# Mixer of a two-layer block: separate VectorE signals, and banded heads normalized by a product with a diagonal in eleven turns

## The chip, the cores and the metric

The kernel runs on one core of one Trainium2 chip. The metric is the device time of one execution in microseconds (us); the time of a version is the median of its timed runs. All data is fp32 (in the large matrix products as pairs of rounded halves).

## What is computed

The program is a chain of two blocks. The first block (a diagonal state space layer, a gating unit, a routed layer of experts) comes first and isn't touched. The second block has two layers; its first layer begins with a mixer of two parts that read the same projections:

```
# part A, delta heads: 4 heads of 128, two directions, 5 chunks of 106 or 104 tokens in this kernel
a_mat = where(strict, (k*beta) @ k.T * decay, 0)          # decay = exp(gc_i - gc_j)
sol   = triangular_solve(I + a_mat, [v*beta, k*beta*exp(gc)])   # u, w
v_new = u - w @ S
o     = (q*exp(gc)) @ S + (q @ k.T * decay) @ v_new
S     = S * exp(gc_last) + k_dec.T @ v_new

# part B, banded heads: 8 heads of 64, 5 query tiles (16 meta tokens, then 4 of 128)
s = q @ k_window.T - slope * dist ; s_meta = q @ k_meta.T ; s_sink
p = softmax([s, s_meta, s_sink])
o = p_window @ v_window + p_meta @ v_meta
```

An output projection, an MLP and a second attention layer with its MLP follow.

## The kernel before

All five engines run one program written out by hand; semaphores join them. The mixer is four generators on each engine: one for each direction `d` of the delta heads and one for each of two banded heads that go side by side (`NWIN` = 2). `mixer_order()` (L1608) gives the order in which every engine advances them, the same on all: 125 steps, each with one turn of direction 0 and one of direction 1, and spread between them 8 x 20 window turns, each for both banded heads. Each of the 5 chunks of a direction takes 25 steps (numbered 0 to 24 here), so that direction 0 goes from the first chunk to the last and direction 1 the other way. A `yield` ends a turn. An engine does its turns strictly in this order: what waits holds up all that is queued behind it on that engine.

One chunk of a direction, by step:
- 0: TensorE sums the log decays and spreads them (L1641 to L1644, banks A and B); VectorE copies them (L2375, L2376), ScalarE takes two Exp (L1999, L2000), VectorE multiplies (L2378).
- 1: TensorE transposes k and v (L1650), ScalarE copies them (L2003, L2004), GpSimd makes vb, kbe and kd (L2265 to L2267).
- 2: VectorE makes the decay exponents Dm and DT (L2385, L2386, eight instructions), ScalarE takes three Exp (L2008 to L2010).
- 3: TensorE multiplies k by k and k by q (L1656, L1658); VectorE multiplies Dm, DT, qd and copies gl (L2394 to L2397), one signal behind them all; TensorE transposes A (L1663); ScalarE copies it (L2013).
- 4: VectorE starts the inverse Xi and its transpose XT (L2401 to L2407), one signal behind both; GpSimd masks A (L2277).
- 5 to 21: six rounds of doubling, each in three steps. TensorE multiplies the masked A by Xi (L1672), ScalarE copies the product T1 (L2018), in the next step TensorE updates (L1678 for Xi, L1681 for XT) and VectorE subtracts (L2414, L2416), one signal behind both. The third step is free.
- 22: U and W (L1686, L1688), copied by ScalarE (L2022, L2023). 23: the state is applied (L1695, L2422). 24: output and new state (L1702 to L1707, L2430 to L2439).

One pair of banded heads, by its 8 turns: 0, scores on TensorE (L1724, or L1727 and L1728). 1, VectorE adds the distance term and takes the maximum (L2457 to L2461). 2, ScalarE Exp with the sum (L2040). 3, VectorE reciprocal (L2465), ScalarE multiplies the weights by it (L2043). 4, TensorE transposes the weights with the identity (L1733, and L1734 for the 16 meta keys). 5, ScalarE copies them (L2047, L2048). 6, value products on TensorE (L1740, L1741). 7, VectorE copies the result out (L2471); the next pair's scores use the same bank and wait for that.

In the rows `GW_value` is the working space of direction 0, `delta` that of direction 1, `held_uH_value` the banded heads' space, `PS` the PSUM banks, `held_C` constants, `BIG` the projections and results. A product of fp32 is recorded as two MATMULs, a transpose as one.

## Time and profile before

| | us |
|---|---|
| median of three timed runs | 3447.63 (3445.48 to 3459.86) |
| the profiled execution's own time | 3457.6 |
| its span, first to last instruction | 3455.8 |
| the mixer in it | 1915 to 2352, 437 |
| busy in the whole span: TensorE, VectorE, ScalarE, GpSimd | 2829.4, 1703.9, 1677.4, 1126.7 |
| mean granted TensorE clock, as a share of 2.4 GHz | 0.871 |

The profile is of one execution. Busy time counts instructions of an engine; "idle before, releaser" is the time an engine stood idle before an instruction and the instruction whose signal let it go. A row that merges several instructions shows their count; the time in it runs from the start of the first to the end of the last, and instructions overlap by some 0.1 us. `PE` is TensorE, `PEld` its weight loads, `DVE` VectorE, `ACT` ScalarE, `POOL` GpSimd.

### The profile page before, as it was taken

How to read it: one execution, taken by the hardware profiler on the slowest of the kernel's cores; microseconds unless marked ns; L12 is line 12 of the kernel's file. 1: busy time of each engine (PE TensorE's matmuls, PEld its weight loads, DVE VectorE, ACT ScalarE, POOL GpSimd, SP SyncE). 2: the span in 40 equal slices, each digit the busy share in tenths (PEclk: the TensorE clock that was granted, in tenths of full speed). 3: DMA queues.
4: the chain of work that ended last, by engine and by line, in shares of the span. 5: the costliest groups of instructions: out<-in, count | busy, mean ns of one | idle time of the engine just before them, and what ended most of it. 6: DMA issues, size and time to landing. Idle time of an engine off the chain costs nothing.

```text
span 3455.8 us, 44071 instructions
## 1 busy us (share of the span) xinstructions
PE 2829.4 (82%) x17284; PEld 2378.8 (69%) x17284; DVE 1703.9 (49%) x3905; ACT 1677.4 (49%) x3352; POOL 1126.7 (33%) x877
## 2 busy tenths in 40 slices
PE   6577777777778776587589888888999999989999
PEld 4465566555656565455387776777999987778887
DVE  7596868685868678355353444543200123621010
ACT  2176676767676867588533232333322322533231
POOL 0033333333333333233132222223555532046463
PEclk8798888788887887589799788978999999999999
DMA  5298999999998999999122000001233321023332
GB/s 183 98 418 333 351 413 407 346 386 405 402 374 353 401 419 408 414 405 388 52 68 68 1 1 1 1 1 50 74 92 92 92 74 56 1 67 95 95 97 74
DMA packets 287522, 695.73 MB, mean 201 GB/s; under 512 B 27664, under 2 KB 207299, under 8 KB 221651
## 3 DMA queue, kind: packets, MB, share of 16 engines
q0 software_dynamic: 73728, 536.90, 38.8%
q1 hardware_dynamic: 213587, 156.02, 14.2%
q8 instruction: 136, 2.23, 0.3%
q14 instruction: 71, 0.58, 0.0%
HBM read 689.72 MB, written 3.15 MB: 200 GB/s over the span
## 4 chain that ended last, share of the span: by engine, by line
PE 54%; DVE 23%; DMA 11%; ACT 10%; issue 3%; POOL 0%; SPq 0%; DVEq 0%; ACTq 0%; POOLq 0%
PE PS L1771 28%; DMA ring<-in_peer_uv,eidx 10%; DVE ring L1494 6%; PE PS L906 5%; ACT ring L1111 3%; PE PS L783 2%; PE PS L960 2%; PE PS L1672 2%; PE PS L1681 2%; PE PS L1678 1%; PE PS L1793 1%; DVE W L1305 1%; DVE acc L2583 1%; PE PS L1970 1%; PE PS L1740 1%
## 5 line engine op out<-in xcount | busy, mean ns | idle before, releaser
L906 PE MATMUL PS<-C,ring 128*128 128x128 f32 x4096 | 711.5, 326 | 358.0 <-ACT ring L1111 357.1
L906 PEld LDWEIGHTS PS<-C,ring 128*128 128x128 f32 x4096 | 564.9, 167 | 521.2 <-ACT ring L1111 477.3
L711 POOL DMA_INDIRECT ring<-in_peer_uv,eidx x512 | 485.9, 949 | 1162.5 <-PE PS L906 982.8
L1494 DVE CUSTOM_DVE_ANT_0 ring<-ring,PS 128x1024 f32<-128x1024 f32 x512 | 619.5, 1215 | 314.2 <-DMA ring<-in_peer_uv,eidx 305.8
L1111 ACT ACTIVATE ring<-ring,act_d 128x512 f32<-128x512 f32 x1024 | 683.5, 714 | 16.7
L1771 PE MATMUL PS<-held_uH,GW 128*128 128x264 f32 (+1 forms) x3008 | 663.2, 315 | 20.8 <-POOL BIG_value L2308 16.8
L2294 POOL TENSOR_TENSOR GW<-held_wr,GW 128x1024 fp32r<-128x1024 f32 x178 | 428.7, 2410 | 437.0 <-ACT GW L2063 437.0
L1771 PEld LDWEIGHTS PS<-held_uH,GW 128*128 128x128 f32 x3008 | 504.4, 194 | 62.6 <-issue 17.4
L1771 PE MATMUL PS<-BIG_value,GW 128*128 128x264 f32 (+1 forms) x1504 | 448.5, 314 | 0.0
L1771 PE MATMUL PS<-hid,GW 128*128 128x264 f32 (+1 forms) x2304 | 366.5, 321 | 0.0
L1771 PEld LDWEIGHTS PS<-hid,GW 128*128 128x128 f32 x2304 | 332.3, 188 | 33.7
L1771 PEld LDWEIGHTS PS<-BIG_value,GW 128*128 128x128 f32 x1504 | 291.9, 194 | 14.8
L2063 ACT CAST GW<-held_wr 128x1024 fp32r<-128x1024 f32 x178 | 185.3, 1043 | 232.0 <-DVE BIG L2534 116.3
L1104 ACT ACTIVATE act_d<-act_d 128x1 f32<-128x1 f32 x512 | 101.7, 199 | 362.1 <-DVE act_d L1494 360.5
L2534 DVE TENSOR_TENSOR BIG<-BIG,PS 128x528 f32<-128x528 f32 (+1 forms) x48 | 33.4, 696 | 394.8 <-PE PS L1771 394.8
L2545 DVE TENSOR_TENSOR value<-BIG,PS 128x528 f32<-128x528 f32 (+1 forms) x64 | 44.5, 696 | 316.9 <-ACT BIG L2118 316.9
L1108 ACT ACTIVATE act_d<-act_d,gate 128x1 f32<-128x1 f32 x512 | 150.8, 295 | 18.8 <-ACT act_d L1104 0.4
L2308 POOL TENSOR_TENSOR hid<-value,hid 128x528 fp32r<-128x528 f32 (+1 forms) x64 | 83.9, 1311 | 132.8 <-ACT hid L2094 132.8
L2118 ACT ACTIVATE BIG<-PS 128x528 f32<-128x528 f32 (+1 forms) x64 | 38.8, 606 | 177.8 <-PE PS L1771 177.8
L2308 POOL TENSOR_TENSOR BIG_value<-BIG,held_uH 128x528 fp32r<-128x528 f32 (+1 forms) x28 | 37.0, 1326 | 168.2 <-ACT held_uH L2094 168.2
L2018 ACT COPY GW_value<-PS 106x424 f32<-106x424 f32 (+1 forms) x30 | 15.3, 511 | 154.6 <-PE PS L1672 154.3
L783 PE MATMUL PS<-BIG,W 128*128 128x512 f32 x192 | 89.6, 604 | 0.0
(478 smaller groups left out, 3850.7 us busy)
## 6 DMA issues: line engine op xcount, KB each, us to landing
held_wr<-in_w_ff SPq DMA_DIRECT2D x128, 512.0 KB, 4.0
wqr<-in_peer_wq SPq DMA_DIRECT2D x32, 512.0 KB
W<-in_peer_wq SPq DMA_DIRECT2D x31, 512.0 KB
held_wr<-in_w_in_ab SPq DMA_DIRECT2D x18, 512.0 KB, 3.8
ring<-in_peer_uv,eidx POOLq DMA_INDIRECT x512, 9.7
BIG<-in_w_in SPq DMA_DIRECT2D x4, 1536.0 KB, 11.5
held_wr<-in_w_qkv_c SPq DMA_DIRECT2D x12, 512.0 KB, 3.8
w_out<-in_w_out SPq DMA_DIRECT2D x1, 4096.0 KB, 18.4
```

The costliest lines, as they stand in the source:

```text
L711: e.indirect_dma_start(out=ring[:, i % RING, :], out_offset=None, in_=pairs, in_offset=bass.IndirectOffsetOnAxis(ap=eidx[:, blk % 2, k:k + ...
L783: ins = e.matmul(z_bank[c], xT[:, k, :], w_in[:, k, 512 * c:512 * c + 512], start=(k == 0), stop=(k == 7))
L906: ins = e.matmul(bank[6 + j // 4][:, j % 4 * P:(j % 4 + 1) * P], row[:, j * P:(j + 1) * P], ident, start=(k == 0 and j % 4 == 0), stop=(k ...
L960: ins = e.matmul((bank[2], bank[5])[c], xT[:, k, :], pg[:, k, 512 * c:512 * c + 512], start=(k == 0), stop=(k == 7))
L1104: e.activation(a, a, ACT.Gelu).then_inc(*n.up(e_gelu))
L1108: e.mul(a, a, gate[:, blk % 2, k:k + 1]).then_inc(*n.up(e_gact))
L1111: e.mul(row[:, c:c + 512], row[:, c:c + 512], a).then_inc(*n.up(e_scaled))
L1494: e.tensor_tensor_reduce(row, row, hn, 1.0, 0.0, ALU.mult, ALU.add, act[:, k:k + 1]).then_inc(*n.up(e_dot))
L1771: ins = e.matmul(bank[b + a][:, 0:w], (hi, lo)[w_][:, k * P:(k + 1) * P], (x_hi, x_lo)[x_][:, c0:c0 + w], start=(first and w_ == 0 and x_ ...
L2063: e.copy(r(wH[i % NS]), wr[:, i % NW].rearrange("p k n -> p (k n)")).then_inc(*up(w_hi))
L2294: e.tensor_tensor(r(wL[i % NS]), wr[:, i % NW].rearrange("p k n -> p (k n)"), wH[i % NS], ALU.subtract).then_inc(*up(w_lo))
L2308: e.tensor_tensor(r(dst), value_, hi, ALU.subtract).then_inc(*up(lo_g))
```

## The change

Delta heads. VectorE signals after line 2394 alone (Dm, which the transpose of A needs); it makes Xi in the same turn, with its own signal, then DT; in the next turn XT, with its own signal, then qd and gl. In the rounds Xi and XT have a signal each. TensorE waits for the one that it reads: line 1672 for Xi, lines 1678 and 1681 for XT, and at the start of a chunk the sums in bank A wait for one signal less than those in bank B. `b7` gets space of its own.

Banded heads. ScalarE's multiplication (L2043) is gone. VectorE makes the diagonal matrix of reciprocals (identity times the column `dn`, into the new `wdg`) right behind the reciprocal, and TensorE multiplies the unnormalized weights by it (four products for three key tiles and the meta keys) in place of the transposes, which transposes and normalizes at once. A pair takes eleven turns: scores 0, VectorE 1, Exp 2, reciprocal and diagonal 3, products 5, copies 6, value products 8, copy-out 9. The 220 window turns are spread over the same 125 steps (`LAG` is 0, so both directions still go side by side).

```diff
--- before.py
+++ after.py
@@ -496,12 +496,13 @@
         w_ = {x: place([P, 4, 106]) for x in ("b1", "b2", "b3", "b4", "b5", "b6", "b8")}
         for x in ("vb", "kbe", "kd", "S", "kt", "vt"):
             w_[x] = place([P, 4, P])
-        w_["b7"], w_["U"], w_["WT"] = w_["b6"], w_["vt"], w_["kt"]
+        w_["b7"], w_["U"], w_["WT"] = in_uh([P, 4, 106]), w_["vt"], w_["kt"]
         w_["c"] = place([P, 5, 8])
         WD.append(w_)
     wsc = in_uh([P, NWIN, 402])
     wPT = in_uh([P, NWIN * 4, P]).rearrange("p (i m) t -> p i m t", i=NWIN)
     wsw = in_uh([P, NWIN, 4])
+    wdg = in_uh([P, NWIN, P])
     ds.close()
     ab.close()
 
@@ -1601,17 +1602,27 @@
 
 
     XP = [0, 25, 51, 77, 103]
-    XV = [0, 13, 27, 41, 55]
-    X_END = XV[4] + 13
+    XV = [0, 19, 39, 59, 79]
+    X_END = XV[4] + 19
+    LAG, ALONE = 0, 1.6
     HEADS = [(t, h) for t in range(5) for h in range(8)]
 
     def mixer_order():
 
         order = []
-        window = 0
-        for i in range(125):
-            order += [("delta", 0), ("delta", 1)]
-            upto = 8 * (len(HEADS) // NWIN) * (i + 1) // 125
+        window, done = 0, 0.0
+        steps = 11 * (len(HEADS) // NWIN)
+        total = 125 - LAG + 2 * LAG * ALONE
+        for i in range(125 + LAG):
+            both = LAG <= i < 125
+            if i < 125:
+                order.append(("delta", 0))
+            if i >= LAG:
+                order.append(("delta", 1))
+            done += 1.0 if both else ALONE
+            upto = min(steps, round(steps * done / total))
+            if i == 124 + LAG:
+                upto = steps
             for _ in range(upto - window):
                 order += [("window", j) for j in range(NWIN)]
             window = upto
@@ -1637,9 +1648,11 @@
             v4 = lambda a: a[0:c, :, 0:c]
             first, last = s == 0, s == 4
             if s:
-                e.wait_ge(x_dve[d], dv)
+                e.wait_ge(x_dve[d], dv - 1)
             e.matmul(A[0:c, 0:4], incl[0:c, 0:c], g, start=True, stop=True)
             e.matmul(A[0:c, 8:12], after[0:c, 0:c], g, start=True, stop=True).then_inc(*up(x_pe[d]))
+            if s:
+                e.wait_ge(x_dve[d], dv)
             for h in range(4):
                 ins = e.matmul(B[:, h * c:(h + 1) * c], g[:, h:h + 1].to_broadcast([c, P]), incl[0:c, 0:c], start=True, stop=True)
             ins.then_inc(*up(x_pe[d]))
@@ -1667,12 +1680,13 @@
             for l in range(1, 7):
                 yield
                 e.wait_ge(x_pool[d], po + 1 + l)
-                e.wait_ge(x_dve[d], dv + 4 + l)
+                e.wait_ge(x_dve[d], dv + 3 + 2 * l)
                 for h in range(4):
                     ins = e.matmul(A[0:c, h * c:(h + 1) * c], MT[:, h], Xi[:, h], start=True, stop=True)
                 ins.then_inc(*up(x_pe[d]))
                 yield
                 e.wait_ge(x_act[d], ac + 4 + l)
+                e.wait_ge(x_dve[d], dv + 4 + 2 * l)
                 if l < 6:
                     for h in range(4):
                         ins = e.matmul(B[0:c, h * c:(h + 1) * c], XT[:, h], T1[:, h], start=True, stop=True)
@@ -1681,7 +1695,7 @@
                     ins = e.matmul(Cb[0:c, h * c:(h + 1) * c], T1[:, h], XT[:, h], start=True, stop=True)
                 ins.then_inc(*up(x_pe[d]))
                 yield
-            e.wait_ge(x_dve[d], dv + 11)
+            e.wait_ge(x_dve[d], dv + 17)
             for h in range(4):
                 e.matmul(A[0:c, h * P:(h + 1) * P], XT[:, h], w_["vb"][0:c, h, :], start=True, stop=True)
             for h in range(4):
@@ -1696,7 +1710,7 @@
                 ins.then_inc(*up(x_pe[d]))
             yield
             if not first:
-                e.wait_ge(x_dve[d], dv + 12)
+                e.wait_ge(x_dve[d], dv + 18)
             for h in range(4):
                 if not first:
                     e.matmul(A[:, h * c:(h + 1) * c], Sx[:, h], qd[:, h], start=True, stop=False)
@@ -1726,19 +1740,23 @@
             else:
                 e.matmul(bk[0:qn, META:META + WK], qB[ps, h % 4, q0:q0 + qn], kB[ps, k0:k0 + WK], start=True, stop=True)
                 e.matmul(bk[0:qn, 0:META], qB[ps, h % 4, q0:q0 + qn], kB[ps, 0:META], start=True, stop=True).then_inc(*up(y_pe[i]))
-            for _ in range(4):
+            for _ in range(5):
                 yield
-            e.wait_ge(y_act[i], 3 * q + 2)
+            e.wait_ge(y_act[i], 2 * q + 1)
+            e.wait_ge(y_dve[i], 2 * q + 2)
+            by = wdg[0:qn, i, 0:qn]
             for m in range(len(tiles)):
-                e.transpose(bk[:, m * P:m * P + qn], s[:, m * P:(m + 1) * P], ident2[0:qn, 0:qn])
-            e.transpose(bk[0:META, 3 * P:3 * P + qn], s[:, WK:WK + META], ident2[0:qn, 0:qn]).then_inc(*up(y_pe[i]))
-            yield
-            yield
-            e.wait_ge(y_act[i], 3 * q + 3)
+                e.matmul(bk[:, m * P:m * P + qn], s[:, m * P:(m + 1) * P], by, start=True, stop=True)
+            e.matmul(bk[0:META, 3 * P:3 * P + qn], s[:, WK:WK + META], by, start=True, stop=True).then_inc(*up(y_pe[i]))
+            yield
+            yield
+            yield
+            e.wait_ge(y_act[i], 2 * q + 2)
             oc = bk[64 * hh:64 * hh + 64, 0:qn]
             for m, tile in enumerate(tiles):
                 e.matmul(oc, vtok[:, tile, 64 * kv:64 * kv + 64], pt[:, m, 0:qn], start=(m == 0), stop=False)
             e.matmul(oc, vtok[0:META, 0, 64 * kv:64 * kv + 64], pt[0:META, 3, 0:qn], start=False, stop=True).then_inc(*up(y_pe[i]))
+            yield
             yield
             yield
 
@@ -2038,17 +2056,13 @@
             yield
             e.wait_ge(y_dve[i], 2 * q + 1)
             e.activation(s[:, 0:W1], s[:, 0:W1], ACT.Exp, bias=nm, accum_out=dn).then_inc(*up(y_act[i]))
-            yield
-            e.wait_ge(y_dve[i], 2 * q + 2)
-            e.mul(s[:, 0:W1 - 1], s[:, 0:W1 - 1], dn).then_inc(*up(y_act[i]))
-            yield
-            yield
+            for _ in range(4):
+                yield
             e.wait_ge(y_pe[i], 3 * q + 2)
             e.copy(pt[:, 0:len(tiles), 0:qn], bk[:, 0:len(tiles) * P].rearrange("p (m t) -> p m t", t=P)[:, :, 0:qn])
             e.copy(pt[0:META, 3, 0:qn], bk[0:META, 3 * P:3 * P + qn]).then_inc(*up(y_act[i]))
-            yield
-            yield
-            yield
+            for _ in range(5):
+                yield
 
     def second_scalar(e, n):
         up, now, nxt = n.up, n.now, n.next
@@ -2391,27 +2405,28 @@
             e.wait_ge(x_pe[d], pe + 4)
             e.wait_ge(x_act[d], ac + 3)
             for h in range(4):
-                e.scalar_tensor_tensor(Dm[:, h], A[0:c, h * c:(h + 1) * c], beta[:, h:h + 1], Dm[:, h], ALU.mult, ALU.mult)
-            e.tensor_tensor(DT, heads(Cb, c, c), DT, ALU.mult)
-            e.tensor_tensor(qd, conv[:, 0:4, c0:c0 + c], EB, ALU.mult)
-            e.tensor_copy(gl, EB[:, :, c - 1 if d == 0 else 0]).then_inc(*up(x_dve[d]))
-            yield
+                ins = e.scalar_tensor_tensor(Dm[:, h], A[0:c, h * c:(h + 1) * c], beta[:, h:h + 1], Dm[:, h], ALU.mult, ALU.mult)
+            ins.then_inc(*up(x_dve[d]))
             Xi, XT, AT = v4(w_["b3"]), v4(w_["b4"]), v4(w_["b5"])
             e.wait_ge(x_dve[d], dv + 4)
             e.tensor_tensor(Xi, Dm, wide(lv[0]), ALU.mult).then_inc(*up(dve))
             e.wait_ge(*n.now(dve))
-            e.tensor_tensor(Xi, wide(ident2), Xi, ALU.subtract)
+            e.tensor_tensor(Xi, wide(ident2), Xi, ALU.subtract).then_inc(*up(x_dve[d]))
+            e.tensor_tensor(DT, heads(Cb, c, c), DT, ALU.mult)
+            yield
             e.wait_ge(x_act[d], ac + 4)
             e.tensor_tensor(XT, AT, wide(lvT[0]), ALU.mult).then_inc(*up(dve))
             e.wait_ge(*n.now(dve))
             e.tensor_tensor(XT, wide(ident2), XT, ALU.subtract).then_inc(*up(x_dve[d]))
+            e.tensor_tensor(qd, conv[:, 0:4, c0:c0 + c], EB, ALU.mult)
+            e.tensor_copy(gl, EB[:, :, c - 1 if d == 0 else 0])
             for l in range(1, 7):
                 yield
                 yield
-                e.wait_ge(x_dve[d], dv + 4 + l)
+                e.wait_ge(x_dve[d], dv + 4 + 2 * l)
                 if l < 6:
                     e.wait_ge(x_pe[d], pe + 4 + 3 * l)
-                    e.tensor_tensor(Xi, Xi, heads(B, c, c), ALU.subtract)
+                    e.tensor_tensor(Xi, Xi, heads(B, c, c), ALU.subtract).then_inc(*up(x_dve[d]))
                 e.wait_ge(x_pe[d], pe + (5 + 3 * l if l < 6 else 22))
                 e.tensor_tensor(XT, XT, heads(Cb, c, c), ALU.subtract).then_inc(*up(x_dve[d]))
                 yield
@@ -2426,7 +2441,7 @@
             ov = oT[:, :, c0:c0 + c]
             other = 4 - s
             if (i > 2) if d == 0 else (i <= 2):
-                e.wait_ge(x_dve[1 - d], XV[other] + (12 if other == 0 else 13))
+                e.wait_ge(x_dve[1 - d], XV[other] + (18 if other == 0 else 19))
                 e.tensor_tensor(ov, ov, heads(A, c), ALU.add).then_inc(*up(x_dve[d]))
             else:
                 e.tensor_copy(ov, heads(A, c)).then_inc(*up(x_dve[d]))
@@ -2461,14 +2476,17 @@
             e.tensor_reduce(nm, s[:, 0:W1], AX.X, ALU.max, negate=True).then_inc(*up(y_dve[i]))
             yield
             yield
-            e.wait_ge(y_act[i], 3 * q + 1)
-            e.reciprocal(dn, dn).then_inc(*up(y_dve[i]))
-            yield
-            yield
-            yield
-            yield
+            e.wait_ge(y_act[i], 2 * q + 1)
+            if q:
+                e.wait_ge(y_pe[i], 3 * q - 1)
+            e.reciprocal(dn, dn).then_inc(*up(dve))
+            e.wait_ge(*n.now(dve))
+            e.tensor_scalar(wdg[0:qn, i, 0:qn], ident2[0:qn, 0:qn], dn, None, ALU.mult).then_inc(*up(y_dve[i]))
+            for _ in range(6):
+                yield
             e.wait_ge(y_pe[i], 3 * q + 3)
             e.tensor_copy(uT[64 * hh:64 * hh + 64, 4 + h // 2, q0:q0 + qn], bk[64 * hh:64 * hh + 64, 0:qn]).then_inc(*up(y_out[i]))
+            yield
             yield
 
     def second_vector(e, n):
```

## Rows read from the trace of the kernel before

**Rows 1.** The mixer as one stretch: us, busy (instructions) by engine, clock, DMA share

```profile
1915.00:2352.00 437.00, 362.74 (x2677) 320.66 (x2678) 209.85 (x612) 131.79 (x361) 93.20 (x90) 0.84 0.00 1
```

**Rows 2.** Waits of TensorE in the mixer, us in total, times, longest

```profile
PE PS L1663 <- DVE GW_value L2397: 21.9, 5, 4.7
PE PS L1733 <- ACT held_uH_value L2043: 18.5, 15, 1.4
PE PS L1663 <- DVE delta L2397: 11.1, 5, 2.2
PE PS L1724 <- DVE BIG L2471: 7.6, 9, 0.9
PE PS L1727 <- DVE BIG L2471: 5.3, 6, 0.9
PE PS L1740 <- ACT held_uH_value L2048: 5.0, 5, 1.1
PE PS L1672 <- DVE delta L2407: 2.0, 4, 0.6
```

**Rows 3.** Timeline of VectorE, third chunk: start us, us, line, count, wait before

```profile
2088.45 0.32 DVE L2385 SCALAR_TENSOR_TENSOR GW_value<-PS,GW_value,held_C 106x106 f32<-106x106 f32 x1
...
2092.21 1.03 DVE L2394 SCALAR_TENSOR_TENSOR GW_value<-PS,bg,GW_value 106x106 f32<-106x106 f32 x4
...
2142.32 0.57 DVE L2461 TENSOR_REDUCE held_uH_value<-held_uH_value 128x1 f32<-128x401 f32 x1
```

**Rows 4.** Timeline of ScalarE, same chunk

```profile
2089.13 0.61 ACT L2004 COPY delta<-PS 106x512 f32<-106x512 f32 x1
...
2093.64 0.62 ACT L2040 ACTIVATE held_uH_value<-held_uH_value 128x401 f32<-128x401 f32 x1
2094.16 0.19 ACT L2040 ACTIVATION_READ_ACCUMULATOR held_uH_value<-held_uH_value 128x1 f32 x1
...
2142.71 0.51 ACT L2018 COPY delta<-PS 106x424 f32<-106x424 f32 x1 [0.23 <-PE PS L1672]
```

**Rows 5.** Timeline of TensorE, same chunk

```profile
2095.31 0.92 PE L1663 MATMUL PS<-held_C,GW_value 106*106 106x106 f32 x4 [4.75 <-DVE GW_value L2397]
...
2139.40 1.61 PE L1724 MATMUL PS<-kB,BIG 64*128 64x400 f32 x4 [0.88 <-DVE BIG L2471]
...
2142.53 0.99 PE L1678 MATMUL PS<-GW_value 106*106 106x106 f32 x8
...
2147.18 0.55 PE L1733 MATMUL PS<-held_C,held_uH_value 128*128 128x128 f32 x3 [1.42 <-ACT held_uH_value L2043]
```

**Rows 6.** Instructions of line 2397: shortest/median/longest ns, first and last start

```profile
L2397 DVE COPY GW_value<-GW_value x5: 999/999/1043, 1926.4 to 2277.3; 128x4 f32<-128x4 f32 x5
L2397 DVE COPY delta<-delta x5: 164/164/164, 1932.6 to 2284.2; 128x4 f32<-128x4 f32 x5
```

**Rows 7.** Timeline of GpSimd, same chunk

```profile
2092.84 1.04 POOL L2266 TENSOR_TENSOR delta<-delta 106x512 f32<-106x512 f32 x1
```

**Rows 8.** Chain that ended last, pieces in order: start us, us, what

```profile
2072.59 0.22 PE PS L1733 x2
...
2073.24 1.75 PE PS L1695 x16
...
2351.93 0.58 PE PS L1740 x4
...
2353.81 1.89 PE PS L1781 x8
```

**Rows 9.** Stretches of low and high clock, columns as in rows 1

```profile
2102.00:2126.00 24.00, 21.80 (x95) 17.85 (x96) 9.88 (x21) 4.47 (x11) 4.62 (x5) 0.50 0.00 1
2126.00:2173.00 47.00, 41.26 (x358) 36.46 (x357) 20.10 (x51) 16.70 (x43) 6.70 (x7) 1.00 0.01 1
2187.00:2201.00 14.00, 7.94 (x40) 7.18 (x40) 9.94 (x22) 5.48 (x15) 4.64 (x5) 0.52 0.00 1
2276.00:2300.00 24.00, 17.76 (x87) 15.23 (x88) 11.35 (x25) 5.86 (x17) 7.54 (x7) 0.51 0.00 1
```

## Prediction

> **What bounds the kernel now.** I read the stretches of the mixer first, then what each engine waited for in it, then the four engines' timelines of one chunk, then the clock. The mixer runs from 1915 to 2352 us, in five chunks of some 87 us, and nothing outside these 437 us is touched. TensorE is busy for 363 of the 437, VectorE for 210, ScalarE for 132 [rows 1]. So TensorE sets the pace, and what can be won is its 74 idle us, plus what it loses at the low clock: the mean grant of 0.84 [rows 1] means that some 0.32 of the 437, 140 us, ran at 1.2 GHz instead of 2.4; all of it at the upper level would give at most half of that, 70 us.
>
> The idle time has few places [rows 2]. Per chunk: one wait of direction 0's transpose of A for VectorE's line 2397 (21.9 us in five, 4.4 each), one of direction 1's (11.1, 2.2 each), three waits of the heads' transposes for ScalarE's normalization (18.5 in 15), three of the scores for VectorE's copy-out (7.6 and 5.3 in 15), one of the value products (5.0 in 5). All engines take the turns in the same written order and strictly one after the other, so a turn can only be early if everything before it on its engine is.
>
> **Signals one by one (delta heads).** Now the transpose of A waits for 2394 to 2397 together. The timelines of a middle chunk show the head: 2394 begins at 2092.21, the transpose of A follows at 2095.31 [rows 3, 5]. With its own signal it follows 2394, which takes 1.03 with the overlap and 0.95 without: direction 0 wins 2.1 us. Of these 1.00 is the copy of 2397, which takes 0.16 in direction 1 [rows 6]; what stands behind 2394 there is then some 1.1 to 1.2, and the wait falls from 2.2 to 1.1: -5.5 us in five chunks. The inverse's own two signals let line 1672 start without XT; it waited 2.0 us in direction 1 [rows 2], and I take that as gone. Later in the rounds a window turn or the other direction covers the update already, so nothing is won there.
>
> **Eleven turns.** 220 window turns are spread over 125 steps instead of 160. Laying both out by the formula: the pattern repeats in every chunk (four pairs of heads in 25 steps) as before. Then:
> - Scores now stand right behind a round's last product or in the next step, with the copy-out a whole round earlier. All 15 waits for 2471 go: -12.9 us [rows 2].
> - The products with the diagonal stand three or more turns behind Exp, and no ScalarE multiplication is between. Of 18.5 us I leave 2 (step 21, where Exp is in step 20 behind both copies): -16.5. The value products have their copy two turns earlier: -5.0.
> - Head of the chunk. Before, step 1 held only the score preparation; VectorE ended it at about 2088.4 and began the decay (2385) at 2088.45 [rows 3]. Now steps 0 and 1 also hold Exp and the reciprocal with the diagonal, *ahead* of the decay on VectorE. Exp stands on ScalarE behind the four copies of k and v, which end at 2089.64 (2089.13 plus a step of 0.51); two Exp at 0.52 plus 0.10 for the read of the sum end at 2090.9 [rows 4]. Then reciprocal and diagonal of the second head, some 0.3 (the trace of before has no such diagonal; its nearest row is a decay instruction of 106x106 with 0.32 [rows 3]; bounds 0.1 and 0.6), so decay starts at 2091.3: 2.9 us late, with decay, its Exp, 2394 and the transpose of A queued behind it. Against it stand the 2.1 won.
> - The diagonals meet GpSimd. Line 2397 of direction 0, a copy of 128x4, takes 1.00 us in every chunk, where GpSimd is in its run of vb, kbe, kd (1.04 each), and direction 1's, with GpSimd idle, 0.16 [rows 6, 7]. A diagonal from SBUF to SBUF in that same run can wait in the same way, 0 to 0.8 each; I take 0.9 for the two. So the first wait goes from 4.75 to 4.75 - 2.1 + 2.9 + 0.9 = 6.5. Over five chunks: +9 (bounds +4 and +13).
> - A new wait in the rounds. In steps 7 and 13 Exp stands on ScalarE *ahead* of the T1 copies of steps 8 and 14 (before, it stood behind them). Scores start at 2139.40; the second head's preparation ends at about 2142.80 (2461 at 2142.32 plus 0.48) [rows 3, 5]; Exp, its sum and the T1 copy (0.52 + 0.10 + 0.51 [rows 4]) make 2143.97, while line 1678 would be free at 2142.53 [rows 5]: 1.5 us. With two tiles of keys instead of three each of these is shorter, and I estimate 1.05; in the chunk of the 16 meta queries 0.8; at the low clock the products hide it. Ten places: 4 x 1.5 + 4 x 1.05 + 2 x 0.8 - 1.5 (one at the low clock) = +10. Bounds 0 and 15.
> - Steps 22 and 23: no head product covers the copies of U and W any longer: +0.3 a chunk, +1.5. Value products stand ahead of the last output instead of behind it: 1.88 us [rows 8] of which about 0.6 was on the path anyway: +1.3.
>
> **The products with the diagonal.** The transposes are replaced by full fp32 products of 128 columns. A transpose takes 0.11 at the upper clock (0.22 for two), and a product of 128 columns 0.218 (16 recorded instructions, eight products, in 1.75) [rows 8]. There are 80 of 128 columns and 32 for the meta keys; those of the 16-query chunk cost nothing to speak of. By the starts in the rounds eight transposes take 1.01 against 1.75 for eight products, so 0.094 each: 112 x 0.094 = 10.5, and the quarter of them that lies at the low clock costs double, +2.7: +13 (bounds 0 if waits absorb them, 16). The ScalarE multiplication that goes (0.5 to 0.6, 40 of them) is worth nothing besides: ScalarE is 30% busy.
>
> Sum at an unchanged clock: -5.5 - 2.0 - 12.9 - 16.5 - 5.0 + 9 + 10 + 1.5 + 1.3 + 13 = **-7 us**.
>
> **The clock.** In the middle chunk the low level lasts from 2102 to 2126 (0.50), behind two waits and two runs of transposes; in the last from 2276 to 2300 (0.51); in the fourth, same program, only 14 us, 2187 to 2201 [rows 9]. The clock thus isn't fixed by the program alone. What the change does to it: after the second transpose of A there are no waits, and lines 1672 and 1678/1681 of the first round follow each other without the value products between them, as they do from 2122 to 2126 where the clock came back. I expect 10 us less of low clock in three chunks, some short falls behind the 0.88 waits to go, and some new ones to come at the 1.5 waits. From 140 us to some 115: half of 25, **-12 us**. Bounds: 80 us of low clock left (-30), 175 (+17).
>
> Against the profiled execution (span 3455.8, time 3457.6) that is 3438.6; the profiled one stands 10 us above the median of the three timed runs, 3447.6, and the change of -19 is carried over to it: **3429 us**.
>
> The Trainium skill has two rules on this. "SBUF — State Buffer", section "SBUF: two separate sides", says that VectorE instructions in a two-port mode or with two SBUF inputs and GpSimd lock one shared port pair for a whole instruction; the trace agrees with the 1.00 against 0.16 of line 2397, and without the rule the first wait would be 5.6 instead of 6.5, 4.5 us less in all. "TensorE: Matmul & The Clock Gate", section "Part 4: PE-mode transpose", says that transposes do not count as activity for the clock gate as products do; that is the rule behind the second rival below. The trace is mixed on it: the level stayed up over the transposes at 2147.18 with a wait of 1.42 us before them [rows 5, 9].
>
> **Rivals.**
> 1. *Forecast*: waits shift as above, clock a little better, -7 to -31 us, 3417 to 3441, likeliest 3429: 0.50.
> 2. *Clock*: the real products and the shorter second wait keep it up, low clock falls to 80 us or less: -7 - 30 = -37, 3411 (3395 to 3417). For: 70 us hang on it, the fourth chunk shows it possible. Against: the longest wait grows from 4.75 to 6.5. 0.15.
> 3. *The moved wait eats it*: diagonals and Exp ahead of the decay cost 13 instead of 9, T1 waits 15 instead of 10, products 16 instead of 13, clock as it was: -7 + 4 + 5 + 3 = +5, with the clock's -12 reduced to 0: 3441 to 3457. 0.25.
> 4. *Slower*: the 1.5 us waits of steps 8 and 14 each let the clock fall for a round, behind which the products run at half speed. Ten rounds of 7 us at the low level cost 3.5 each, +35, less those where it is low already: -7 + 35 = +28, 3476. It makes the kernel slower from the third such round on, and by more than 0.5% from the seventh. For: TensorE then stands idle 1.5 of some 7 us. Against: waits of 1.42 in the middle chunk did no such thing [rows 5, 9]. 0.08.
> 5. *No effect of the kind claimed*: an in-order neighbour keeps all waits, +13 for products and nothing won: 3461. The timelines leave little room: 0.02.
>
> **How the numbers follow.** About 0.5% (17 us) is what a measurement of this kernel tells from no change. Faster by more needs below 3430.4: case 2 and six tenths of case 1, 0.45. Slower by more, above 3464.9: case 4 and part of 5, 0.09. The rest, 0.46. The range must leave out no more than 0.2: 3402 to 3455, from the middle of case 2 to near the end of case 3.
>
> **What would show it.** Right: the wait of line 1663 for direction 0 about 6 us, with line 2385 of a chunk starting only behind the reciprocal; 2471 no longer a releaser of TensorE; line 1678 waiting 1 to 1.5 us for ScalarE's 2018 some eight times; line 1672 not waiting for VectorE; eight products of a head pair in 1.75 at the upper clock. Wrong: if line 1663's wait falls instead of rising, if the mean grant of the mixer leaves 0.84 by more than 0.04 either way, or if the time moves outside the mixer.

## The result: 38 us faster, all of it in the mixer

| | before | after |
|---|---|---|
| median, us (four timed runs each) | 3450.19 (3445.48 to 3459.86) | 3411.99 (3407.37 to 3417.59) |
| ratio, 95% interval | | 0.9892 (0.9862 to 0.9923) |
| profiled execution, time and span | 3457.6, 3455.8 | 3410.21, 3408.1 |
| mixer, from the first sum of decays to the last output of a direction | 1915.0 to 2352.6 = 437.6 | 1906.3 to 2306.1 = 399.8 |
| mean granted clock of the whole span | 0.871 | 0.887 |

The forecast was 3429 with a range of 3402 to 3455, from a median of 3447.6: -19. Measured is -38: right side, inside the range, twice the size. 3412 lies in the range of the second rival (3395 to 3417, chance 0.15), not in that of the likeliest case (3417 to 3441, 0.50). The mixer alone became 37.8 us shorter. That it starts 9 us earlier has nothing to do with the change, since no instruction ahead of it moved; from run to run the start lies between 1905 and 1915. So below, the length of the mixer is what is compared, beside the medians.

The mixer of after as one stretch answers [rows 1] (columns as there), the second line is that of before over its exact length:

```profile
1906.30:2306.10 399.80, 348.53 (x2816) 305.12 (x2816) 230.32 (x653) 114.77 (x321) 90.06 (x90) 0.93 0.00 1
```

```profile
1915.00:2352.60 437.60, 363.33 (x2681) 321.09 (x2682) 210.41 (x612) 131.79 (x361) 93.20 (x90) 0.84 0.00 1
```

TensorE issues 135 more recorded matmuls and is nevertheless busy 15 us less, because the clock was granted at 0.93 instead of 0.84.

TensorE's waits in the mixer of after (us in total, times, longest), to be read against [rows 2]. Line 1676 is the transpose of A (1663 before), 2408 the product that makes Dm (2394), 1692 the update of Xi (1678), 2036 the copy of T1 (2018), 1757 the value products (1740):

```profile
PE PS L1676 <- DVE GW_value L2408: 30.7, 5, 6.2
PE PS L1692 <- ACT GW_value L2036: 10.2, 10, 1.4
PE PS L1676 <- DVE delta L2408: 5.6, 5, 1.1
PE PS L1757 <- ACT held_uH_value L2063: 1.3, 1, 1.3
...
PE PS L1749 <- DVE held_uH_value L2484: 0.5, 2, 0.2
```

The waits for the copy-out and for ScalarE's normalization are gone. The wait for direction 0's decay grew from 21.9 to 30.7, and the ten new waits for T1 are there.

**One account for all runs.** In each kernel's profile the mixer's length is split in three, so that the parts add up to it: TensorE's idle time; the work, which is its busy time less half of the busy time that fell into stretches of low clock, that is, what the same products would take at 2.4 GHz; and that half, the cost of the low clock. The low stretches of before and after, cut at the ends of the mixer and listed in order with their sum (us of the stretches, TensorE busy in them):

```profile
...
1928.20:1945.30 17.10, 12.77 (x71) 0.50 0.00 1
...
2102.30:2126.20 23.90, 22.00 (x97) 0.50 0.00 1
2187.60:2201.30 13.70, 8.24 (x41) 0.50 0.00 1
2245.70:2252.50 6.80, 6.80 (x39) 0.51 0.01 2
2276.40:2300.30 23.90, 18.06 (x89) 0.50 0.00 1
...
sum 140.00, PE 118.09; mean PE 8.44
```

```profile
...
1990.60:2000.80 10.20, 7.22 (x34) 0.50 0.00 0
2069.10:2075.90 6.80, 3.11 (x18) 0.50 0.00 1
2154.40:2161.30 6.90, 3.83 (x20) 0.51 0.00 0
2239.80:2246.60 6.80, 3.81 (x20) 0.50 0.00 0
sum 54.70, PE 38.59; mean PE 4.82
```

| profile | mixer | idle | work | low clock's cost | low clock, us |
|---|---|---|---|---|---|
| before | 437.6 | 74.3 | 304.3 | 59.0 | 140 |
| after | 399.8 | 51.3 | 329.2 | 19.3 | 55 |
| difference | -37.8 | -23.0 | +24.9 | -39.7 | -85 |

Fewer waits just about pay for the products; what is left over is the clock. In the last three chunks of after it falls only once each, at the head, and half of that stretch is a time in which TensorE waits anyway. Each line is one execution, and the low clock differs between executions: in experiment 11, whose waits are those of after, it is 61 us instead of 55, and in experiment 4, whose waits are those of before, 123 instead of 140. The medians stand beside it for that reason.

### The profile page after: what moved, and what is told of

Its sections match the earlier page's. It is cut to its first block and busy times, and to the rows that moved or that the text cites. A ratio compares the mean times of both kernels' runs of the same rounds, so it can differ in the third digit from the quotient of the medians.

```text
span 3408.1 us, 44465 instructions
## 1 busy us (share of the span) xinstructions
PE 2796.5 (82%) x17412; PEld 2349.9 (69%) x17412; DVE 1724.6 (51%) x3945; ACT 1662.8 (49%) x3312; POOL 1125.8 (33%) x877
## 5 line engine op out<-in xcount | busy, mean ns | idle before, releaser
L1789 PE MATMUL PS<-held_uH,GW 128*128 128x264 f32 (+1 forms) x3008 | 662.3, 315 | 20.6 <-POOL BIG_value L2322 16.5
L850 PE MATMUL PS<-W,wqr 128*128 128x128 f32 x512 | 81.7, 314 | 5.4 <-DMA wqr<-in_peer_wq 4.6
```

The source lines that it names most:

```text
L850: ins = e.matmul(bk[:, half * P:(half + 1) * P], query_slot(i)[:, k * P:(k + 1) * P], hnT[:, k, :], start=(k == 0), stop=(k == 7))
L1789: ins = e.matmul(bank[b + a][:, 0:w], (hi, lo)[w_][:, k * P:(k + 1) * P], (x_hi, x_lo)[x_][:, c0:c0 + w], start=(first and w_ == 0 and x_ ...
```

## The experiments

Two theories of the clock stood against each other: that it followed the waits (W) and that it followed real products in place of transposes (P).

**1. The delta heads' part alone.** The changed kernel with the banded heads and the order of before.

```diff
-            for _ in range(5):
-                yield
-            e.wait_ge(y_act[i], 2 * q + 1)
-            e.wait_ge(y_dve[i], 2 * q + 2)
...
-                e.matmul(bk[:, m * P:m * P + qn], s[:, m * P:(m + 1) * P], by, start=True, stop=True)
...
+            for _ in range(4):
+                yield
+            e.wait_ge(y_act[i], 3 * q + 2)
...
+                e.transpose(bk[:, m * P:m * P + qn], s[:, m * P:(m + 1) * P], ident2[0:qn, 0:qn])
...
```

> The delta heads of the changed kernel (a signal each for line 2394, Xi and XT) with the banded heads of the kernel before (8 turns, normalized by ScalarE, transposed with the identity). Both theories: TensorE's first wait for the decay falls from 21.9 us (five) to about 11, the second from 11.1 to about 5.6, the others stay: -18 us. Theory W (the clock follows the waits): the low clock of the mixer falls well below 140 us, to some 100, and the time is 3450 - 18 - 20 = about 3412. Theory P (the clock follows real products in place of transposes): the low clock stays near 140 us and the time is about 3432.

Measured: 3415.69 (before on the same chip 3445.06), ratio 0.9898 (0.9864 to 0.9932). Mixer 406.4 = 60.7 idle + 304.8 work + 40.9 for 85 us of low clock. TensorE's waits (1667 is the transpose of A, 1738 that of the heads' weights):

```profile
PE PS L1738 <- ACT held_uH_value L2048: 22.4, 15, 1.9
PE PS L1667 <- DVE GW_value L2399: 11.1, 5, 2.7
PE PS L1729 <- DVE BIG L2477: 7.6, 9, 0.9
PE PS L1667 <- DVE delta L2399: 7.4, 5, 2.1
```

The first wait is halved as expected; the second lost 3.7 instead of 5.5, and 3.9 came back in front of the heads' transposes. No transpose was replaced here, and the low clock still went from 140 to 85 us: for W. This part alone is measured as fast as the whole change (0.9898 against 0.9892, with intervals of 0.003).

**2. The banded heads' part alone.** Before with eleven turns and the products with the diagonal, the delta heads' signals as before. Its lines against the changed kernel:

```diff
-    XV = [0, 19, 39, 59, 79]
+    XV = [0, 13, 27, 41, 55]
...
-                ins = e.scalar_tensor_tensor(Dm[:, h], A[0:c, h * c:(h + 1) * c], beta[:, h:h + 1], Dm[:, h], ALU.mult, ALU.mult)
-            ins.then_inc(*up(x_dve[d]))
+                e.scalar_tensor_tensor(Dm[:, h], A[0:c, h * c:(h + 1) * c], beta[:, h:h + 1], Dm[:, h], ALU.mult, ALU.mult)
...
```

> The banded heads of the changed kernel (eleven turns, products with the diagonal) with the delta heads of the kernel before. Waits by both theories: the first wait for the decay grows from 4.4 to about 8.2 us a chunk (+19), the second stays at 2.2, those for copy-out, normalization and copies go (-34), ten new ones of 1 to 1.5 us for the T1 copies (+10), the products cost +12: +9 us in all with the ends. Theory P: the low clock falls to some 60 us, -35, time about 3425. Theory W: low clock stays at 130 to 150 us, time about 3459.

Measured: 3434.72, ratio 0.9968 (0.9948 to 0.9989). Mixer 418.9 = 63.2 idle + 328.8 work + 26.9 for 72 us of low clock. The first wait took 36.2 us (41 expected), the ten for T1 10.2. The time lies between the theories: the products cost 24 us of work, twice the expectation, and the low clock fell nearly as P said (some 60), while W had said 130 to 150. Alone this doesn't tell whether the products did that or the 34 us of waits that went.

**3 and 4. The products by themselves, out of the one and into the other.** The changed kernel with transposes (the weights stay unnormalized), and the kernel before with products by the identity.

```diff
-                e.matmul(bk[:, m * P:m * P + qn], s[:, m * P:(m + 1) * P], by, start=True, stop=True)
+                e.transpose(bk[:, m * P:m * P + qn], s[:, m * P:(m + 1) * P], ident2[0:qn, 0:qn])
...
```

> The changed kernel with its products with the diagonal turned back into transposes with the identity; waits, turns and the diagonal on VectorE stay, only the normalization of the banded heads' weights is left out of the result. Both: 12 us less of TensorE work. Theory P: the low clock goes back to 120 to 140 us, time 3412 - 12 + 35 = about 3435. Theory W: the low clock stays at 55 to 70 us, time about 3400.

```diff
-                e.transpose(bk[:, m * P:m * P + qn], s[:, m * P:(m + 1) * P], ident2[0:qn, 0:qn])
+                e.matmul(bk[:, m * P:m * P + qn], s[:, m * P:(m + 1) * P], ident2[0:qn, 0:qn], start=True, stop=True)
...
```

> The kernel before with its transposes of the banded heads' weights turned into full products with the identity; nothing else. Both: +12 us of TensorE work, waits as before. Theory P: low clock falls from 140 to some 60 us, time 3450 + 12 - 35 = about 3427. Theory W: low clock as before, time about 3462.

Measured: 3396.00, ratio 0.9835 (0.9800 to 0.9870), mixer 383.3 = 54.1 + 306.5 + 22.7 (61 us of low clock); and 3466.97, ratio 1.0053 (1.0035 to 1.0071), mixer 451.6 = 71.7 + 327.6 + 52.3 (123 us). So with transposes the changed kernel keeps its high clock, and with products the kernel before keeps its low one: P falls. W stands in 1, 3 and 4, but not as it was stated for 2, where the first wait grew to 36 us in all and the low clock was halved nevertheless: which waits and what work stand between them matters, and not the long wait alone. And the products cost some 23 us of work whichever way it is measured (329.2 - 306.5 = 22.7, 327.6 - 304.3 = 23.3); the medians moved by 16 and 22, the 16 across two chips on which the kernel before took 3450.19 and 3445.06.

**5 and 6. The moved wait at the head.** In 5, Exp, reciprocal and diagonal, products and copies each stand one turn later; in 6 only the decay exponents are moved, one step earlier.

```diff
             yield
             yield
+            yield
             e.wait_ge(y_dve[i], 2 * q + 1)
             e.activation(s[:, 0:W1], s[:, 0:W1], ACT.Exp, bias=nm, accum_out=dn).then_inc(*up(y_act[i]))
-            for _ in range(5):
+            for _ in range(4):
                 yield
...
```

> The changed kernel with Exp, reciprocal and diagonal, the products and their copies each one turn later (turns 3, 4, 6, 7 of eleven). Theory: Exp then stands behind the T1 copies of ScalarE in every round, and reciprocal and diagonal behind the decay at the head. The ten waits for T1 (10.2 us) go, the first wait for line 2408 falls from 30.7 us (6.1 each) to about 20, the others stay: about 3412 - 21 = 3391, a little less if the low clock shrinks with it. Rival (the long wait is of the delta chain alone and turns don't matter, or other waits take the place): 3405 or more.

```diff
             e.tensor_tensor(bge, egc, beta, ALU.mult).then_inc(*up(x_dve[d]))
             yield
-            yield
             Dm, DT = v4(w_["b1"]), v4(w_["b2"])
...
             ins.then_inc(*up(x_dve[d]))
             yield
+            yield
```

> The changed kernel with VectorE's decay exponents (lines 2399 and 2400) in the step before, ahead of the reciprocal and diagonal instead of behind them; nothing else moved. Theory (the moved wait of the prediction: Exp and diagonals ahead of the decay): the first wait falls from 6.1 to about 3.7 us a chunk, -12 us, time about 3400; the T1 waits stay at 10.2. Rival: the wait is set by ScalarE's order, it stays above 5.5 and the time within 4 us of 3412.

Measured: 3405.27, ratio 0.9883 (0.9852 to 0.9914), mixer 385.3 = 34.5 + 327.0 + 23.7; and 3404.97, same ratio and interval, mixer 392.2 = 42.8 + 329.0 + 20.4. The waits of experiment 5 did what was expected, but for the last line:

```profile
PE PS L1676 <- DVE GW_value L2408: 20.0, 5, 4.4
PE PS L1676 <- DVE delta L2408: 6.3, 5, 1.8
PE PS L1749 <- DVE held_uH_value L2485: 5.8, 5, 1.2
```

The T1 waits are gone there, and 5.8 us came in for the diagonals. In 6 the first wait is 22.0, 4.4 each where 3.7 was expected, and the T1 waits stay at 10.2. So Exp and diagonals ahead of the decay were what lengthened that wait. The mixers became 14.5 and 7.6 us shorter; of the medians, 7 each, only the second matches. Both times missed the expectation (3391 and 3400), and that of 5 is the one that its rival named. A difference of 7 us lies inside the intervals, and the kernel before took 5.5 us less on this chip than on that of the result, so the medians don't show a gain; the waits in the profiles do.

**7 and 9. Work in the wait.** Products of the identity with itself that nobody reads, ahead of direction 0's transpose of A: 24 in the changed kernel, 12 with the turns of experiment 5.

```diff
+            if d == 0:
+                h0 = 4 * s
+                e.wait_ge(y_dve[0], 2 * h0 + 1)
+                for _ in range(24):
+                    e.matmul(bank[6][:, 0:P], ident2, ident2, start=True, stop=True)
             e.wait_ge(x_dve[d], dv + 4)
```

> The changed kernel with 24 added products of the identity with itself (128 columns, 5.3 us at the upper clock), which nobody reads, ahead of direction 0's transpose of A in each chunk, where TensorE waits 6.1 us. They cost nothing at the upper clock. Theory (the clock falls because TensorE stands idle there): the low clock shrinks from 55 us to under 25, and with some 19 us hanging on it the time falls to about 3400. Rival (the clock falls for another cause): the low clock stays and the time is 3412 to 3418.

> The turns of e5_exp_later and 12 added products (2.7 us at the upper clock) in the shorter wait at the head. If both theories hold: the waits of e5_exp_later filled, low clock under 25 us, about 3380. If idle time isn't what the clock follows: as e5_exp_later, 3391.

Measured: 3406.56, ratio 0.9889 (0.9858 to 0.9920), mixer 395.4 = 25.2 idle + 356.5 work (of which the added products are 26) + 13.7 for 27 us of low clock, all of it in the first two chunks; and 3387.54, ratio 0.9840 (0.9807 to 0.9872), mixer 373.6 = 21.4 idle + 342.0 work (of which the added products are 13) + 10.2 for 20 us of low clock. Filling the wait removes the fall of the clock behind it in the last three chunks of both. In 7 that shortened the mixer by 4.4 us, where 12 were expected: half of each low stretch had lain in the wait itself, where a low clock costs nothing. The median is 5 us lower, as much as the chips differ. 9 is to be compared with 5, from the same chip and with the same turns: 3387.54 against 3405.27, with no overlap of their runs (3382.68 to 3393.70, 3402.85 to 3405.65), the mixer 11.7 us shorter (idle time 13.1 less, work 15.0 more, the clock's cost 13.5 less). That is the cleanest measure of what filling brings.

Idle time isn't all that the clock follows. At the end of the first chunk it fell in 9 behind a wait of only 0.4 us (in 7 behind one of 1.3), and stayed low for 17 us in which TensorE was never idle:

```profile
1966.90:1983.90 17.00, 17.00 (x78) 0.50 0.00 1
```

What it follows there was not tried.

**8 and 10. The same in the kernel before.** In 8 eighteen added products in the first wait; in 10 nine more in the second and five ahead of each pair's transposes.

```diff
+            e.wait_ge(y_dve[0], 8 * s + 1)
+            for _ in range(9 if d else 18):
+                e.matmul(bank[6][:, 0:P], ident2, ident2, start=True, stop=True)
             e.wait_ge(x_dve[d], dv + 4)
...
+            if i == 0:
+                e.wait_ge(y_dve[i], 2 * q + 1)
+                for _ in range(5):
+                    e.matmul(bk[:, 0:P], ident2, ident2, start=True, stop=True)
             e.wait_ge(y_act[i], 3 * q + 2)
```

> The kernel before with 18 added products of the identity with itself (4.0 us at the upper clock), which nobody reads, in the first of the two waits for line 2397 of each chunk (4.4 us); all else as before. Theory (the clock follows idle stretches of TensorE at the head of a chunk, both of them): low clock falls from 140 us to 60 to 110, the second waits of 2.2 and 1.1 us stay empty; time 3445 - 15 to - 35, some 3425. Rival (the head's idle time has nothing to do with it): low clock 125 us or more, time 3445 to 3450.

> The kernel before with added products that nobody reads in both waits at the head (18 and 9) and ahead of every pair's transposes (5, 1.1 us at the upper clock); the waits themselves stay, TensorE only works in them. Theory (the long low stretches follow a run of waits with little work between them: the second wait for line 2397, the transpose, the wait for the normalization): with all of them filled the low clock shrinks from 109 us with the first wait filled, and 140 with none, to under 60; the time falls to about 3420. Rival (the clock follows something else than idle time): low clock 100 us or more, time 3450 or more.

Measured: 3450.93, ratio 1.0011 (0.9995 to 1.0027), mixer 434.1 = 56.8 + 326.4 + 50.9 for 109 us of low clock; and 3447.17, ratio 0.9998 (0.9980 to 1.0016), mixer 442.0 = 36.7 + 359.0 + 46.4 for 96 us. Both expectations of some 3420 to 3425 were wrong. In 8 the added products (20 us) just fill what the first wait loses (21.9 to 2.1), and the clock's cost falls by only 8 us. In 10 idle time falls by 37.6 and the clock's cost by 12.7, but the work grows by 54.7. Part of that excess is plain: 5 of the 20 pairs had no wait ahead of their transposes, and the added products there come to 5.5 us. The timeline of TensorE at the head of the third chunk of experiment 10 (1666 is the transpose of A, 1675 the first product of a round, 1747 the value products; the wait before a row in brackets) shows another part:

```profile
2094.66 0.57 PE L1666 MATMUL PS<-held_C,delta 106*106 106x106 f32 x4 [0.19 <-DVE delta L2404]
...
2097.84 0.96 PE L1675 MATMUL PS<-GW_value 106*106 106x106 f32 x8 [0.30 <-DVE GW_value L2414]
2100.82 1.55 PE L1675 MATMUL PS<-delta 106*106 106x106 f32 x8 [2.01 <-DVE delta L2414]
2102.30 1.54 PE L1747 MATMUL PS<-held_uH_value,vtok 128*64 128x128 f32 x6
```

The two waits and that for the normalization are filled, and now the first product of a round in direction 1 waits 2.0 us for line 2414, the end of XT; over the mixer these waits grew from 2.9 us to 13.0 (10.0 and 3.0). At the upper clock TensorE reaches that point sooner than VectorE's chain of four instructions per direction (direction 1's transpose of A begins at 2094.66, the product that waits at 2100.82); before, the low clock and the waits ahead had hidden it. Behind this wait the clock fell again:

```profile
2101.00:2113.00 12.00, 11.12 (x57) 0.57 0.01 1
```

So time that the low clock costs is not all won where another chain is the next bound, and half of the busy time in low stretches is only an upper bound of what hangs on the clock. The changed kernel has no such wait, since there the first product of a round waits for Xi alone. That its own signal is worth more than the 2.0 us of [rows 2] when the clock is high is thus likely, but not shown: in experiment 2, with the signals of before and 72 us of low clock, these waits came to 0.8. Whether the low clock of before would be gone with this wait filled too was not tried.

**11 and 12. The width of the stationary matrix.** In 11 the second head of a pair does its product for the 16 meta keys first; 12 is experiment 9 with this order in both the products with the diagonal and the value products.

```diff
+            if i:
+                e.matmul(bk[0:META, 3 * P:3 * P + qn], s[:, WK:WK + META], by, start=True, stop=True)
             for m in range(len(tiles)):
-                e.matmul(bk[:, m * P:m * P + qn], s[:, m * P:(m + 1) * P], by, start=True, stop=True)
-            e.matmul(bk[0:META, 3 * P:3 * P + qn], s[:, WK:WK + META], by, start=True, stop=True).then_inc(*up(y_pe[i]))
+                ins = e.matmul(bk[:, m * P:m * P + qn], s[:, m * P:(m + 1) * P], by, start=True, stop=True)
+            if not i:
+                ins = e.matmul(bk[0:META, 3 * P:3 * P + qn], s[:, WK:WK + META], by, start=True, stop=True)
+            ins.then_inc(*up(y_pe[i]))
```

> The changed kernel; the second head of each pair does its product for the 16 meta keys ahead of its wide ones, so that the stationary matrix changes its width twice per pair instead of four times; same work. Theory (a product costs 0.22 us and each change of width some 0.09 more, which the prediction left out): a pair with three key tiles takes 2.1 instead of 2.29 us, about 3.5 us less in all. Rival (the extra is of the products themselves): 2.29 as before.

> e9_both with the order of e11_meta_first in the products with the diagonal and the same in the value products. If each change of width costs 0.09 us: 7 us less than e9_both (3387.5), about 3381, waits and low clock as there. If not: 3387.

A pair's products with three key tiles, TensorE's timeline, in after and in experiment 11 (1749 and 1750 the wide and the narrow ones of after; 1751, and 1753 or 1749 those of the experiment), each followed by the next group:

```profile
2077.91 0.85 PE L1749 MATMUL PS<-held_uH_value 128*128 128x128 f32 x6
2078.69 0.39 PE L1750 MATMUL PS<-held_uH_value 128*16 128x128 f32 x2
2079.01 0.94 PE L1749 MATMUL PS<-held_uH_value 128*128 128x128 f32 x6
2079.88 0.39 PE L1750 MATMUL PS<-held_uH_value 128*16 128x128 f32 x2
2080.20 0.87 PE L1757 MATMUL PS<-held_uH_value,vtok 128*64 128x128 f32 x6
```

```profile
2082.64 0.85 PE L1751 MATMUL PS<-held_uH_value 128*128 128x128 f32 x6
2083.42 0.39 PE L1753 MATMUL PS<-held_uH_value 128*16 128x128 f32 x2
2083.65 0.38 PE L1749 MATMUL PS<-held_uH_value 128*16 128x128 f32 x2
2083.96 0.94 PE L1751 MATMUL PS<-held_uH_value 128*128 128x128 f32 x6
2084.82 0.87 PE L1761 MATMUL PS<-held_uH_value,vtok 128*64 128x128 f32 x6
2085.62 0.43 PE L1762 MATMUL PS<-held_uH_value,vtok 16*64 16x128 f32 x2
2085.98 0.87 PE L1761 MATMUL PS<-held_uH_value,vtok 128*64 128x128 f32 x6
```

From start to start the pair takes 2.29 us in after and 2.18 in the experiment. The narrow product followed by another narrow one takes 0.23, the one followed by a wide one 0.31: a product of 128 columns is 0.22, as the prediction took it, and such a change of the stationary matrix's shape adds 0.09. Four of them are 0.36 of the 0.5 us that the pair takes beyond eight times 0.22. A further 0.1 lies in the wide group that follows a narrow one: three wide products take 0.78 us in the first group of a pair and 0.87 in the second (2077.91 to 2078.69, 2079.01 to 2079.88). The pair had four changes and now has three, not two as the expectation said: the last wide product stands before one of another width all the same. Width alone isn't it: in the value products the stationary matrix keeps its 64 columns and changes from 128 rows to 16, and the narrow one takes 0.36 instead of 0.22 (2085.62 to 2085.98). And a change between 128 and 106 rows costs nothing, 0.22 to 0.23 from one product to the next (same run):

```profile
2060.70 0.39 PE L1716 MATMUL PS<-delta 128*128 128x106 f32 x2
2060.93 0.39 PE L1717 MATMUL PS<-delta 106*128 106x106 f32 x2
2061.15 0.39 PE L1716 MATMUL PS<-delta 128*128 128x106 f32 x2
```

The timed difference of 11 (3408.03, ratio 0.9895, two runs) is too small to tell. Experiment 12 measured 3378.92, ratio **0.9818 (0.9794 to 0.9842)**, mixer 360.7 = 21.8 idle + 332.1 work + 6.8 for 14 us of low clock:

```profile
1907.80:2268.50 360.70, 338.89 (x2936) 304.82 (x2936) 224.47 (x653) 114.35 (x321) 91.84 (x90) 0.98 0.01 1
```

Against experiment 9, of which it differs by the order alone, the mixer is 12.9 us shorter, 9.9 of it work and 3.4 the clock; 7 were expected. The medians (3387.54 and 3378.92) are of two chips, and the intervals of the ratios overlap. It is 67 us under the kernel before by the medians (3446.05 on its chip), where the change brought 38.

## Why the prediction was right, and where it was off

- **Signals of the delta heads.** Right in size: the first wait's -2.1 a chunk is seen in experiment 1 (21.9 to 11.1 in five), and the second wait came to 5.6 as forecast. The 2.0 for line 1672 were right too, as waits of before; that this wait can grow with the clock (to 13 in experiment 10) was not seen.
- **Copy-out, normalization, value products.** -12.9 as forecast; -18.0 instead of -16.5 (0.5 left, not 2); -3.7 instead of -5.0, since one of the five waits stayed at 1.3.
- **The head of a chunk.** Forecast 6.5 for the first wait, +9 in all; measured 6.2 and +8.8. The steps are all there in the timelines of a middle chunk: ScalarE's last Exp of the heads, VectorE's two diagonals (2484), the decay (2399) behind them, and TensorE's transpose of A:

```profile
2066.81 0.21 ACT L2058 ACTIVATION_READ_ACCUMULATOR held_uH_value<-held_uH_value 128x1 f32 x1
```

```profile
2064.01 0.57 DVE L2476 TENSOR_REDUCE held_uH_value<-held_uH_value 128x1 f32<-128x401 f32 x1
2066.45 0.16 DVE L2482 RECIPROCAL held_uH_value<-held_uH_value 128x1 f32<-128x1 f32 x1 [1.87 <-ACT held_uH_value L2058]
2066.65 0.38 DVE L2484 TENSOR_SCALAR held_uH_value<-held_C,held_uH_value 128x128 f32<-128x128 f32 x1
2067.06 0.17 DVE L2482 RECIPROCAL held_uH_value<-held_uH_value 128x1 f32<-128x1 f32 x1
2067.26 0.76 DVE L2484 TENSOR_SCALAR held_uH_value<-held_C,held_uH_value 128x128 f32<-128x128 f32 x1
2067.95 0.32 DVE L2399 SCALAR_TENSOR_TENSOR GW_value<-PS,GW_value,held_C 106x106 f32<-106x106 f32 x1
```

```profile
2072.79 0.95 PE L1676 MATMUL PS<-held_C,GW_value 106*106 106x106 f32 x4 [6.17 <-DVE GW_value L2408]
```

VectorE had ended the preparation at about 2064.5 and stood 1.87 us for Exp with the decay queued behind it. Experiment 6, which moves the decay ahead, takes 1.7 of the 6.2 us away and so shows the cause. The diagonals' meeting with GpSimd, 0.9 us in the forecast, cost 0.6: 0.38 and 0.76 against 0.28 where GpSimd is idle. In the rounds the first of a pair, which falls into GpSimd's masking of A, takes 1.08 and the second 0.29:

```profile
2108.06 1.01 POOL L2291 TENSOR_TENSOR delta<-delta,held_C 106x424 f32<-106x424 f32 x1
```

```profile
2108.07 1.08 DVE L2484 TENSOR_SCALAR held_uH_value<-held_C,held_uH_value 128x128 f32<-128x128 f32 x1
...
2109.25 0.29 DVE L2484 TENSOR_SCALAR held_uH_value<-held_C,held_uH_value 128x128 f32<-128x128 f32 x1
```

The diagonal begins with GpSimd's instruction and ends just behind it. The Trainium skill, "SBUF — State Buffer", section "SBUF: two separate sides", says that a VectorE instruction in a two-port mode and one of GpSimd take the same port pair for a whole instruction each and that the later one waits; the trace agrees, with 1.08 against 0.29; in which mode the diagonal runs no row shows.
- **The T1 waits.** +10 forecast, 10.2 measured in exactly ten places, 1.4 the longest. Experiment 5 removes them by putting Exp behind the copies.
- **Steps 22 and 23, last output.** +1.5 forecast for the copies of U and W; four waits of 0.2, 0.9 in all, are there, where before one wait of 0.9 stood at the output. The +1.3 at the last output was not measured by itself.
- **The products.** A step that failed: +13 with a bound of 16, from 1.75 us for a pair with three key tiles; it takes 2.29, and the work grew by 24.9. The price per product (0.22) was right for products of one shape, as in the row that it came from (1695). The changes of shape were missing, 0.09 each and four per pair, though the value products of before already showed more than 0.22 (0.58 for two in [rows 8]).
- **The clock.** The larger step that failed: -12 forecast with a bound of -30, -39.7 measured in the account. The prediction named as a sign of being wrong that the mixer's mean grant leaves 0.84 by more than 0.04; it is 0.93. Direction and places were right (low clock between the head and the first rounds), the size was that of the second rival (low clock down to 80 or less, chance 0.15; it is 55), whose reason was half wrong: experiments 3 and 4 show that the products did little for it (61 against 55 us, 123 against 140). The Trainium skill, "TensorE: Matmul & The Clock Gate", section "Part 4: PE-mode transpose", which says that transposes don't count for the clock as products do, had been the base of that rival; the runs show no such effect of a size that matters here.
- **The sum.** Waits -20 forecast and -23 measured, products +13 and +25, clock -12 and -40: -19 and -38. With the clock as forecast the change would have come out at -10; with the products as forecast and the clock as measured, at -50, some 3398 and outside the range. Both terms left their own bounds, in opposite directions: that the time lies inside the range is in part luck. What held are the waits, one by one.
- **Slower, the fourth rival,** did not happen: in the last three chunks no 1.4 us wait in the rounds was followed by a fall of the clock.

**What is shown and what is not.** Shown: the low clock goes with the waits and the order of work, not with the kind of instruction (1, 3, 4); the fall behind the long wait goes when TensorE works in it (7, and 9 against 5, in the last three chunks). Only argued: that the long low stretches of before come from two waits shortly behind each other at the head. Filling the waits there (8, 10) moved the low clock from 140 to 109 and 96 us, less than this would ask for; in 10 a new wait of 2 us stood at the place, in 8 there was none of that size. Which of the change's parts keeps the clock up is open beyond this: each alone does much of it (85 and 72 us against 55 together).

## What to carry to other kernels

Where engines take turns in one written order, list for each step what stands *ahead* of the critical instruction on its own engine after the change: that gave each new wait here to within 0.3 us, and two of them could be taken back by moving single turns. Split the time of a stage into idle time, work at the full clock and the cost of the low clock; a change of waits is worth more than its waits when the clock hangs on them, but only as far as the next chain allows. And price a product by what stands beside it, not by its columns alone. Filling a wait with products that nobody reads pays only where the wait is, and only as long as they fit into it.

## What the runs showed of the hardware that was not expected

Between fp32 products a change of the stationary matrix from 128 to 16 or 64 columns or back, or from 128 to 16 rows, costs TensorE 0.09 us at the upper clock (0.31 against 0.22 to 0.23 us from one product to the next) and up to 0.1 more in the first product behind it (0.87 against 0.78 for three); one between 128 and 106 rows costs nothing. Products that nobody reads cost next to nothing in a wait (experiment 7: 26.1 us less idle, 27.3 more work) and kept the clock at 2.4 GHz behind it in the last three chunks of the changed kernel, though not in the one before. The clock can also fall and stay low for 17 us of unbroken work (experiment 9). Transposes in place of products (61 against 55 us of low clock) made next to no difference to the clock. A diagonal of 128x128 on VectorE takes 0.28 us, and up to 1.08 where a GpSimd instruction is under way.
